# Two transposes of each layer norm between the next stage's first products, and the key search's results transposed four blocks earlier

## What is computed

```
for l in 0, 1:                               # first block
    y = concat(mixer_l(x), memory_attention(x)) @ w_out[l]
    x = layer_norm(alpha*x + y)              # norm x1 (l=0), x3 (l=1)
    q = x @ w_q                              # 8 heads, two halves each
    s = q . sub_keys                         # 128 keys per half
    top 16 of each half, top 16 of their sums -> 128 of 16384 experts, softmax gate
    f = sum over those experts of gelu(x . u[e]) * gate * v[e]
    x = layer_norm(alpha*x + f)              # norm x2, x4
for l in 0, 1:                               # second block
    x = layer_norm(alpha*x + mixer2_l(x))    # norm x4m, x5
    x = layer_norm(alpha*x + moe(x))         # norm x5m, x6; 16 experts, a router picks two
```

## Time and profile before

| | |
|---|---|
| Time, median of 3 runs | 3052.53 us (3047.21 to 3054.27) |
| The profiled execution, its own time | 3049.17 us |
| Its span | 3047.3 us |
| Granted PE clock, mean | 0.981 |
| PE busy | 2937.4 us (96%) |
| DVE busy | 1978.6 us (65%) |
| ACT busy | 1320.3 us (43%) |
| POOL busy | 314.8 us (10%) |

### The profile page before, as it was taken

How to read it: one execution, slowest core, us unless ns; L and a number is a source line. 1 busy time by engine, 2 the same in 40 slices (tenths; PEclk the granted TensorE clock), 3 DMA queues, 4 the chain that set the end, 5 groups by cost and what they waited for, 6 DMA issues and landing times.

```text
span 3047.3 us, 47641 instructions
## 1 busy us (share of the span) xinstructions
PE 2937.4 (96%) x19441; PEld 2621.9 (86%) x19441; DVE 1978.6 (65%) x3831; ACT 1320.3 (43%) x2130; POOL 314.8 (10%) x178
## 2 busy tenths in 40 slices
PE   7989999999999998999999999999999999999998
PEld 7779999998888897999999888878668997878997
DVE  4567968965556647697897555566675546465455
ACT  3333544445555334354544455533433333443332
POOL 0004920000000001394000000001000000010000
PEclk9999999999999999999999999998999999999999
DMA  5234544445556543354444555555035555325553
GB/s 194 98 133 139 177 149 160 157 163 193 194 193 205 186 156 111 124 177 158 157 156 170 183 193 194 193 179 144 12 99 166 174 185 171 125 76 164 177 180 118
DMA packets 224137, 478.83 MB, mean 157 GB/s; under 512 B 27168, under 2 KB 109104, under 8 KB 223920
## 3 DMA queue, kind: packets, MB, share of 16 engines
q1 hardware_dynamic: 220960, 473.29, 46.6%
q10 hardware_dynamic: 2960, 2.49, 0.3%
HBM read 474.14 MB, written 1.57 MB: 156 GB/s over the span
## 4 chain that ended last, share of the span: by engine, by line
PE 88%; DVE 7%; ACT 2%; POOL 2%; issue 1%; DMA 0%; SPq 0%; DVEq 0%; ACTq 0%; POOLq 0%
PE ps L133 87%; POOL ring_rest L148 2%; DVE big L156 2%; DVE spl L148 1%; PE ps L136 1%; DVE xb L156 1%; DVE st L172 1%; ACT big L139 1%; DVE xr L148 1%; DVE st L156 0%; DVE big L148 0%; ACT spl L139 0%; ACT whi L139 0%; POOL big L148 0%; ACT L139 0%
## 5 line engine op out<-in xcount | busy, mean ns | idle before, releaser
L139 ACT ACTIVATE whi<-ring 128x1024 fp32r<-128x1024 f32 x512 | 542.5, 1060 | 691.5 <-PE ps L133 691.3
L133 PE MATMUL ps<-xr,whi 128*128 128x256 f32 x4096 | 752.9, 286 | 10.9 <-POOL ring_rest L148 10.2
L148 DVE TENSOR_TENSOR ring_rest<-ring,whi 128x1024 fp32r<-128x1024 f32 x412 | 503.6, 1223 | 323.0 <-ACT whi L139 323.0
L133 PEld LDWEIGHTS ps<-xr,whi 128*128 128x128 f32 x4096 | 643.2, 193 | 13.8 <-DVE big L178 8.6
L133 PE MATMUL ps<-xr,spl 128*128 128x256 f32 (+1 forms) x5256 | 644.6, 285 | 9.3 <-DVE xr L148 5.4
L133 PEld LDWEIGHTS ps<-xr,spl 128*128 128x128 f32 (+1 forms) x5256 | 640.0, 192 | 13.9 <-DVE xr L148 5.8
L133 PE MATMUL ps<-whi,Ar 128*128 128x512 f32 x2048 | 633.6, 391 | 4.5 <-DVE Ar L148 4.5
L148 DVE TENSOR_TENSOR spl<-ring,spl 128x1024 fp32r<-128x1024 f32 (+3 forms) x384 | 426.9, 1162 | 297.0 <-ACT spl L139 296.5
L133 PE MATMUL ps<-xr,ring_rest 128*128 128x256 f32 x2048 | 582.2, 284 | 0.0
L133 PEld LDWEIGHTS ps<-whi,Ar 128*128 128x128 f32 x2048 | 386.1, 189 | 85.2 <-DVE Ar L148 5.0
L133 PE MATMUL ps<-ring_rest,Ar 128*128 128x512 f32 x1024 | 399.9, 390 | 0.0
(11 more groups left out here) (109 smaller groups left out, 2320.2 us busy)
## 6 DMA issues: line engine op xcount, KB each, us to landing
ring<-in_peer_u_dram SPq DMA_DIRECT2D x256, 512.0 KB, 3.3
ring<-in_peer_v_dram SPq DMA_DIRECT2D x256, 512.0 KB, 3.5
ring<-in_moe_w_gate_dram SPq DMA_DIRECT2D x64, 512.0 KB, 4.2
ring<-in_moe_w_up_dram SPq DMA_DIRECT2D x64, 512.0 KB, 5.3
ring<-in_moe_w_down_dram SPq DMA_DIRECT2D x64, 512.0 KB, 4.4
ring<-in_peer_w_q_dram SPq DMA_DIRECT2D x32, 512.0 KB, 4.4
ring<-in_sb_w_in_dram SPq DMA_DIRECT2D x24, 512.0 KB, 4.8
ring<-in_ab_w_in_dram SPq DMA_DIRECT2D x20, 512.0 KB, 6.3
```

The lines of the kernel that those rows point to most:

```text
L133: return self.e.matmul(o, l, r, start=start, stop=stop)
L139: return self.e.activation(o, i, f, **k)
L148: return self.e.tensor_tensor(o, a, b, op)
```

## The change

Two edits, both of order alone; no instruction is added or taken out. First, in a norm PE transposes quarters 0 and 1 only. The two fillers and the transposes of quarter 2 stand behind chunk 1 of the next stage's first products, and those of quarter 3 behind chunk 3. Second, `("res", 0)` stands after 46 blocks instead of 50, so that four blocks lie between the transposes of the search results and the first gate event. `BEFORE` stays 50, and the lists of DVE, ACT, POOL and SP keep their order.

```diff
--- before.py
+++ after.py
@@ -456,7 +456,11 @@
                 for i in range(4):
                     for n, o in outs:
                         ins = column(n, o, i)
+                    if p == 0 and i < 3:
+                        between_pe(pe, xk, i)
                 ins.then_inc(*psum.next(((pr["name"], g), "used")))
+                if p == 0:
+                    between_pe(pe, xk, 3)
                 return
             for n, o in outs:
                 for i in range(4):
@@ -723,10 +727,18 @@
             for t, h in ((0, 0), (0, 1), (1, 0), (1, 1)):
                 give(pe, 2 * t + h, (vec, (name, "sum", t, h)))
             busy(pe, 20)
-            for q in range(4):
-                turn_pe(pe, name, xb, q, 4 + q, [(vec, (name, "x", q, 1))])
-                if q < 3:
-                    busy(pe, 2)
+            for q in range(2):
+                norm_turn_pe(pe, name, q)
+
+        def norm_turn_pe(pe, name, q):
+            if q:
+                busy(pe, 2)
+            turn_pe(pe, name, xb, q, 4 + q, [(vec, (name, "x", q, 1))])
+
+        def between_pe(pe, name, c):
+
+            if c in (1, 3) and name in NORMS:
+                norm_turn_pe(pe, name, c // 2 + 2)
 
         def norm_act(act, name):
             for q in range(4):
@@ -1188,7 +1200,7 @@
 
 
         BEFORE = 50
-        EVENTS = [("h", n) for n in range(BEFORE)] + [("res", 0)]
+        EVENTS = [("h", n) for n in range(BEFORE - 4)] + [("res", 0)] + [("h", n) for n in range(BEFORE - 4, BEFORE)]
         n_ = BEFORE
         for m_ in range(32):
             EVENTS.append(("gate", m_))
@@ -1979,6 +1991,7 @@
                 pe.wait_ge(*vec.at((xk, c // 2)))
                 pe.wait_ge(*lo.at((("rt", l), c // 4)))
                 ins = mm3(pe, ps[0:20, 0, 0:T], [a[:, c % 4, :] for a in w[c // 4]], xs(c), c == 0, c == 7)
+                between_pe(pe, xk, c)
             ins.then_inc(*psum.next((("rt", l), "used"), ("logits", l)))
             give(pe, 0, (acted, ("logits", l)))
             take(pe, 1)
```

## The result

The changed kernel took 3023.23 us, the median of four runs (3019.4 to 3025.94), beside 3052.86 us (3047.21 to 3054.27) for the kernel before: a ratio of 0.9905 with a 95% interval of 0.9888 to 0.9923. That is 29.6 us off where 14.6 were forecast, and it lies outside the range of 3030 to 3046. The direction was right, the size was half of what came.

A forecast was written before the change was run, and what follows sets the result against it. The prediction took PE's unbroken chain of work as the bound, with waits ahead of it. Search results 9.8 us plus norms 4.8 us gave 14.6 off the median 3052.53, so 3037.9, say 3038 us; range 3030 to 3046.

The forecast's parts named there:

- So each place gains between 4.69 (the recorded wait) and 4.97 (the hole by starts). I take 4.9: 9.8 us for two.: Search results, two places: four blocks fill PE's hole before the first gate event, 4.9 us each, 9.8 us off.
- the chain is PE alone for 258.93 us, so nothing gives it back: Behind the first gate event only PE bounds the time, for 258.93 us, so the search results' gain stays.
- The table chain, 4.9 to 9.8 us, hidden: DVE's one-hot tables beside POOL take 4.9 to 9.8 us, ending by 409.3, before the gates are due at 411.1.
- The passage on the shared port: At DVE's tables: six two-input instructions could wait for POOL pieces, up to 7 us, eating 0.4 us; not put in the sum.
- Transposes without a wait for `res`, remainders of blocks 50 to 52 in time: Search results are there 4.5 us before their earlier transposes; DVE's remainders for blocks 50 and 51 aren't late.
- Norms, 4.8 us: Seven norms: the next stage's products fill PE's waits before quarters 2 and 3, 4.8 us off in sum, ends -1 and +8.
- The new wait of 0.9 us: At norms, PE waits 0.9 us for `xr`, as only six products follow quarter 3's transposes before the first needing it.
- the hole opens again: Rival: PE waits at block 50 instead, for late tables or remainders; gain 4.8 us or less, 3048 us; chance 0.10.
- slower, the clock: Rival: PE stays at half clock through 48 products of x1, x3, x4 and x5m, 23.0 us lost, 3064 us; chance 0.05.
- The waits only move: Rival: at norms, late quarter 3, its new wait and half-clock products eat the 4.8 us; gain 9.8, 3043 us; chance 0.17.
- Products among the transposes, as a page's rule: At norms: products replacing waits among transposes would bring the clock back sooner, +1 to +3 us on the sum.

The follow-up runs named there:

- res_only: Kernel before with only the new event list (search results transposed after 46 blocks, norms as before): 3031.28 us, ratio 0.9945.
- fill_hole: Kernel before plus 40 unread products behind the search results' transposes, both blocks, so PE is busy through the wait for the tables: 3047.15 us, ratio 0.9993.
- norms_only: Changed kernel with the old event list, so the kernel before with the norms' edit alone: 3043.03 us, ratio 0.9977.
- res_48: Kernel before with the search results transposed after 48 blocks, two ahead of the gates, norms as before: 3036.09 us, ratio 0.9953.

## Why the forecast was wrong, step by step

- **"So each place gains between 4.69 (the recorded wait) and 4.97 (the hole by starts). I take 4.9: 9.8 us for two."** This is the step that failed, a term of the sum that was mis-sized. The mechanism was right: no wait, gates at 412.74. As the price of the wait alone 9.8 was near (9.1 in `res_only`). But the traces have 13.3 us (`res_only`) to 14.4 for the two places, because the wait's cost went on behind it: the gate stretches ran 4.25 us (2.73 + 1.52) longer than without the hole, and `fill_hole` gets 3.6 of that back with the hole still there. The sentence behind the step, "the chain is PE alone for 258.93 us, so nothing gives it back", was true as far as it went, yet I read "PE alone" as "PE at its pace". The gate events' own rows held the sign: the same 16 products in 1.89 and in 1.64 us.
- **What this step doesn't explain.** With 4.3 us more the forecast would have been 18.9 us off, 3033.6 us, still inside the range, and the changed kernel came out 10.4 us under that. 3.5 us of it is the base: the forecast starts from 3052.53 us, the median of three runs, where 43 later ones have 3049.07. The rest is in stretches that the change doesn't touch, 3 to 5 us in the traces, and at the norms, 1 to 3 us more than forecast. That it is there is shown by the stretches; why the change brings it is open (see below).
- **The table chain, 4.9 to 9.8 us, hidden.** Right, and the trace came out at 9.1; the margin of PE was 2.6 us and not the 6.6 of the lower bound. The passage on the shared port counted the instructions with two inputs alone, and one of the two that paid was a cast, with 1.94 of the 4.2 us.
- **Transposes without a wait for `res`, remainders of blocks 50 to 52 in time.** Right: no wait for either appears.
- **Norms, 4.8 us.** The size was right, 5.75 in the traces and 5.6 in whole runs of `norms_only`, the single terms less so: x1 0.85 (1.0), x2 0 (1.5), x3 0.65 (0.1), x4 3.37 (0.9), x4m 0.26 (0.4), x5m 0.62 (0.7); x5's 0.2 can't be told within its stretch of 1.94. x2 is full clock before and half clock after: its windows from 1027 to 1034 are 1.00 and 0.76, which took the gain; x4 was the reverse. In the changed kernel's second profile x2's stretch was 167.48 and in `norms_only` 167.47, as forecast 1.5 less. So that the sum came out near 4.8 is partly luck: half clock took x2's 1.4 us and gave x4 1.5. How coarse such terms are shows in `res_only`, which has the old norms: its six stretches are 1.9 us shorter than those of before in sum, x4m's alone 2.49 shorter and x2's 1.36 longer.
- **The new wait of 0.9 us.** 0.71 us at x1, x2, x3 and x5m, 0.59 behind x4m and x5.
- **Rival "the hole opens again":** no, by the waits. **Rival "slower, the clock":** no; the clock came back at all norms, and PE didn't stay at half clock through the 48 products of any. **"The waits only move":** no, the waits for `xb` fell 7.8 us while those for `xr` rose 4.1.
- **Products among the transposes, as a page's rule** (the Trainium skill, "TensorE: Matmul & The Clock Gate", "Part 4: PE-mode transpose"), +1 to +3 us: no run here separates it; x4 came out both ways with the same instructions.
- **The range.** It held the bounds of the terms and a scatter of 5 us for the runs, but not that half-clock stretches come and go in the whole rest of the kernel. A value pass differs by 1.5 us between kernels that don't differ there, and x5 to the end by 3.4 (`res_only` and `res_48`).

What stays open: why the changed kernel and its variants have a mean clock of 0.983 to 0.990 run after run, while the kernel before is spread from 0.979 to 0.985. The lost time behind the two holes, 4.7 us by the windows, is 4.7 / 3047 = 0.0015 of mean clock, of the 0.004 to 0.005 between the two kernels. That single stretches fall either way from one execution to the next is shown; why the changed kernel's fall well so steadily is not. The products now running through the old holes and behind the norms' first quarters may be the reason, but no run held everything else still.

## What to carry to other kernels

A wait of PE costs its length and, behind it, what PE loses at the lower clock: read the granted clock in windows of a few microseconds just behind each wait that a change removes, and compare one instruction's duration there with the same one elsewhere. In a kernel with a dozen waits of 2 to 5 us, as here, half-clock stretches come and go in stages that an edit doesn't touch, by 1.5 us in a value pass and up to 3.4 us in the last stretch, and two kernels with the same local gain had medians 4.8 us apart, with runs that overlap; an edit worth less than that is judged by its own stretch, and the range of a forecast needs this scatter on top. Mean clock over a whole run isn't the goal either: fillers in waits raised it without a gain in time that could be told. Filler products that seem useless once work stands ahead of them are worth a run before they are taken out: alone, taking them out came out 3.6 us slower, and together with earlier transposes 3.7 us faster.

## What the runs showed of the hardware

- A hole of about 5 us in an otherwise full PE was followed by up to 8 us of unbroken work at a granted 0.62, some 6 us of it at half clock. With 40 products in the hole it was 1.00.
- A wait of 2.3 us was followed by half clock in one execution and by full clock in another, with the same busy time in the window (6.3 and 6.2 of 8.50 us).
- A VectorE cast of 128x256 took 2.23 us beside a GpSimd piece of 2.40 and 0.29 alone; a table of 1024 half-words took 2.90 beside one and 0.69 alone. A cast of 128x256 that reads from PSUM (`ps`) took 0.42 us beside a GpSimd piece and 0.42 alone.
- Removing half clock where PE would wait anyway gave nothing that could be told: mean granted clock 0.989 to 0.990 instead of 0.987 and 0.988, and medians of 3020.70 and 3021.20 us.
- The profile page's line of forty slices shows nothing of this: each slice is 76 us long, and it reads 9 in nearly all of them before and after.
